# PEER block on one core: another division of the first choosing, gates stored in 16 pieces, and 47 chunks of the second u table split ahead of their use

## The reference, cut to what matters

```python
PEER_HEADS = 8; PEER_NK = 128; PEER_N = 16384; PEER_TOPK = 16; D_MODEL = 1024
def peer_ffn(h, wq, k1, k2, u, v):
    q = (ht @ wq).reshape(n_tok, PEER_HEADS, PEER_QDIM)
    s1 = einsum('thd,kd->thk', q[..., :128], k1); s2 = einsum('thd,kd->thk', q[..., 128:], k2)
    t1, i1 = top_k(s1, 16); t2, i2 = top_k(s2, 16)
    cand_s = (t1[..., :, None] + t2[..., None, :]).reshape(n_tok, 8, 256)
    top_s, pos = top_k(cand_s, 16)                    # 16 of 16384 experts for each token and head
    idx = take_along_axis(i1*128 + i2, pos); g = softmax(top_s)
    act = gelu(einsum('td,thkd->thk', h, u[idx]))     # u, v: 16384 rows of 1024
    return einsum('thk,thkd->td', g * act, v[idx])
```

## The kernel before

| | first layer | second layer |
|---|---|---|
| dense tiles | 4 | 3 |
| pre, ahead, beside | 16, 12, 16 | 16, 17, 19 |
| dots in the first choices, in one tile's 16 steps, in one later choice | 14, 44, 22 | 24, 24, 16 |
| gates of one tile are stored in | 4 pieces of 2 MB | 4 pieces of 2 MB |

## Time and profile before

### The profile page before, as it was taken

How to read it: one execution, slowest core, us unless ns; L and a number is a source line. 1 busy time by engine, 2 the same in 40 slices (tenths; PEclk the granted TensorE clock), 3 DMA queues, 4 the chain that set the end, 5 groups by cost and what they waited for, 6 DMA issues and landing times. The chain is left out here.

```text
span 4329.8 us, 59390 instructions
## 1 busy us (share of the span) xinstructions
PE 3731.4 (86%) x19545; PEld 1931.0 (45%) x19545; DVE 3186.7 (74%) x6186; ACT 1332.3 (31%) x1722; POOL 1663.6 (38%) x1191
## 2 busy tenths in 40 slices
PE   6888779789988898599999978877989888699996
PEld 1555565454434343344444424434545455344442
DVE  2547654539878788689999976843689788588887
ACT  0326521221212121222333305831334334333331
POOL 0400000230323232367887811203344344277774
PEclk8999989899999999899999989988999999899998
DMA  4946754596999998899999962212588797799995
GB/s 205 345 163 221 233 155 152 194 317 212 324 356 322 346 350 333 312 364 403 404 404 404 404 235 72 74 64 84 188 291 304 273 345 244 290 344 341 347 343 219
DMA packets 416426, 1188.55 MB, mean 275 GB/s; under 512 B 40112, under 2 KB 126960, under 8 KB 409584
## 3 DMA queue, kind: packets, MB, share of 16 engines
q1 hardware_dynamic: 240956, 639.75, 41.2%
q0 software_dynamic: 110592, 402.70, 25.7%
q10 hardware_dynamic: 64708, 143.91, 8.6%
HBM read 988.98 MB, written 197.23 MB: 274 GB/s over the span
## 5 line engine op out<-in xcount | busy, mean ns | idle before, releaser
L2097 PE MATMUL ex_R<-ex_vl,hh 128*128 128x512 f16 x1792 | 683.0, 381 | 0.0
L1665 PE MATMUL ca_A<-hh,ca_us 128*128 128x512 f16 x2048 | 634.3, 386 | 50.5 <-ACT ca_ga L1706 39.3
L2097 PE MATMUL ex_R<-hl,hh 128*128 128x512 f16 x1792 | 543.5, 382 | 93.8 <-DVE hh L2111 72.3
L1633 POOL DMA_INDIRECT ca_ug<-in_peer_u_rows,chosen_rows x288 | 293.9, 1020 | 660.6 <-DVE ca_ug L1790 538.7
L2128 DVE SCALAR_TENSOR_TENSOR ex_sum<-ex_vg,ex_share,ex_sum 128x1024 f32<-128x1024 f32 x384 | 493.4, 1285 | 9.8 <-DVE ex_share L2120 6.0
L2025 POOL DMA_INDIRECT ex_vg<-in_peer_v_rows,ex_index x384 | 388.5, 1012 | 190.3 <-issue 85.0
L1706 ACT ACTIVATE ca_ga<-ca_A 128x512 f32<-128x512 f32 (+1 forms) x256 | 139.4, 544 | 897.1 <-PE ca_A L1665 710.9
L1665 PE MATMUL ca_A<-hh,ca_uh 128*128 128x384 f16 x1024 | 345.5, 337 | 77.2 <-DVE ca_ul L1760 32.5
L1790 DVE SCALAR_TENSOR_TENSOR ca_ug<-ca_ug,ca_hp 128x1024 f32<-128x1024 f32 x288 | 346.7, 1216 | 84.4 <-DMA ca_ug<-in_peer_u_rows,chosen_rows 82.5
L1665 PE MATMUL ca_A<-hl,ca_us 128*128 128x512 f16 x1024 | 394.8, 386 | 0.0
L2136 DVE TENSOR_TENSOR ACC<-ACC,ex_R 128x512 f32<-128x512 f32 x448 | 305.8, 683 | 92.5 <-PE ex_R L2097 89.5
(11 more groups left out here) (384 smaller groups left out, 7126.4 us busy)
## 6 DMA issues: line engine op xcount, KB each, us to landing
ex_vr<-in_peer_v SPq DMA_DIRECT2D x256, 512.0 KB, 9.1
ca_us<-u_parts SPq DMA_DIRECT2D x128, 512.0 KB, 6.4
ca_ur<-in_peer_u SPq DMA_DIRECT2D x128, 512.0 KB, 5.2
gates<-ca_stage ACTq DMA_DIRECT2D x28, 2048.0 KB, 16.3
acts<-ca_ga ACTq DMA_DIRECT2D x128, 256.0 KB, 6.1
ex_gr<-gates SPq DMA_DIRECT2D x32, 1024.0 KB
ex_ar<-acts SPq DMA_DIRECT2D x128, 256.0 KB, 11.9
acts<-ca_ga ACTq DMA_DIRECT2D x128, 192.0 KB, 4.0
```

What stands on the lines that cost most here:

```text
L1633: nc.gpsimd.indirect_dma_start(ug[x % UG][:, :], None, u_rows, bass.IndirectOffsetOnAxis(ap=chosen_rows[:, x:x + 1], axis=0)).then_inc(ug_ ...
L1665: last = nc.tensor.matmul(A[b][:, a:a + w], lhs[:, k, :], rhs[:, k, a:a + w], start=(k == 0 and x == 0), stop=(k == KD - 1 and x == 2))
L2097: last = nc.tensor.matmul(R[(NP * q + y) % BANKS][:, :], lhs[q][:, x, o:o + P], rhs[q][:, x, h * 512:h * 512 + 512], start=(x == 0 and n = ...
```

## The change

Numbers of the schedule, in the first layer: `pre` 24 (was 16), `ahead` 11 (12), `beside` 15 (16); dots 20 in the second choice and 26 in the third (14 in the third), then 42 in a gate phase (44) and 14 in a choice phase (22). In the first choice that has dots, they begin when a fifth of its work is done. The places at which scores are loaded and exponentials made move by one to four chunks. In both layers `PARTS` is 16: pieces of 512 KB, spread over all the `ahead` chunks of a choice phase.

In the second layer 47 of the 128 chunks (x from 4 on with x % 8 in 0, 4, 6) are split ahead: 27 in `project_and_norm` n1 (5, 5, 5, 5, 3, 2, 2 in its 7 turns) and 20 in `peer_scores` (1, 1, 2, five times over). `choose_and_activate` loads those as pairs from DRAM, after the chunk that used the buffer before has been multiplied. Of the 81 others 4 are prefetched as before, and DVE subtracts all other 77; POOL subtracts none and only gathers. The prefetch of the 4 is issued by SP behind the stores of the split. Both SP's and ACT's loops in the second choosing are written out.

```diff
-    def __init__(self, nc, io, parts, first, raw, cut, raw_in, high_made, low_made, stored):
+    def __init__(self, nc, io, parts, layer, first, raw, cut, raw_in, high_made, low_made, stored):
+        self.chunks = READY[layer]
...
+READY = (range(PCH), [x for x in range(4, PCH) if x % 8 in (0, 4, 6)])
+SPLIT_NORM1 = (5, 5, 5, 5, 3, 2, 2)
+SPLIT_SCORES1 = (1, 1, 2) * 5
...
-                        rows.move(sp, 0, SPLIT_NORM, SPLIT_NORM)
-                        rows.all_stored(sp, SPLIT_NORM)
+                        rows.move(sp, 0, sum(split), sum(split))
+                        rows.all_stored(sp, sum(split))
...
-                        if rows is not None and i < SPLIT_NORM:
-                            rows.high(act, i)
+                        for x in range(sum(split[:i]), sum(split[:i + 1])) if rows is not None else ():
+                            rows.high(act, x)
...
+                        behind = 1 if tag == "n0" else 0
+                        for x in range(sum(split[:max(0, i - behind)]), sum(split[:i + 1 - behind])) if rows is not None else ():
+                            rows.low(dve, x)
...
-LOW_BY = (None, ("gpsimd", "vector", "gpsimd", "vector"))
...
+                    for j in range(SPLIT_RING if layer == 0 else 0):
+                        sp.dma_start(ring.us[j][:, :, :, :].rearrange("p x k n -> p (x k n)"), parts[j].rearrange("p x n -> p (x n)")).then_inc(ring.u_in[j], 16)
+                    for j in range(0 if layer == 0 else RING):
                         sp.dma_start(ring.ur[j][:, :, :], io["peer_u"][layer][j].rearrange("p (k n) -> p k n", k=KD)).then_inc(ring.u_in[j], 16)
+                    rows.all_stored(sp, upto[-1])
...
-PRE = (16, 16)
+PRE = (24, 16)
...
-    ahead, beside, midway_at = {4: (12, 16, 8), 3: (17, 19, 10)}[nt]
+    ahead, beside, midway_at = {4: (11, 15, 9), 3: (17, 19, 12)}[nt]
-    PARTS = 4
+    PARTS = 16
-    FIRST_DOTS, by_step, BY_CHOICE = {1: (24, [1, 2] * (STEPS // 2), 16), 2: (14, [3, 3, 2, 3] * (STEPS // 4), 22)}[NG]
+    first_dots, by_step, BY_CHOICE = {1: ((24,), [1, 2] * (STEPS // 2), 16), 2: ((20, 26), [3, 3, 2, 3, 2, 3, 2, 3] * (STEPS // 8), 14)}[NG]
...
-                        if last is not None and x % 2 == 0 and x // 2 < PARTS:
-                            store(last, x // 2)
+                        if last is not None:
+                            for part in range(PARTS * x // ahead, PARTS * (x + 1) // ahead):
+                                store(last, part)
...
+                    for x in range(RING, PCH):
+                        j = x % RING
+                        if x in ring.number:
+                            sp.wait_ge(first_done, x + 1)
+                            sp.dma_start(us[j][:, :, :, :].rearrange("p x k n -> p (x k n)"), parts[ring.number[x]].rearrange("p x n -> p (x n)")).then_inc(u_cut[j], 16)
+                            continue
+                        if x < 2 * RING:
+                            sp.wait_ge(first_cut, j + 1)
+                        else:
+                            sp.wait_ge(u_cut[j], ring.cut_upto[x - RING])
+                        sp.dma_start(ur[j][:, :, :], u_src[x].rearrange("p (k n) -> p k n", k=KD)).then_inc(u_in[j], 16)
...
-                        if low_by[j] == "gpsimd":
-                            pool.wait_ge(u_split, k * split_upto[-1] + split_upto[j])
-                            pool.wait_ge(first_done, k * RING + j + 1)
-                            nc.gpsimd.tensor_tensor(ul[j][:, :, :], ur[j][:, :, :], uh[j][:, :, :], ALU.subtract).then_inc(u_cut[j], 1)
...
-                        if not ready and low_by[j] == "vector" and not (isinstance(n, int) and n * CT + x < RING):
-                            dve.wait_ge(u_split, n * (CT // RING * split_upto[-1]) + (x // RING * split_upto[-1] + split_upto[j]))
+                        if not ready and n * CT + x >= RING and n * CT + x not in ring.number:
+                            dve.wait_ge(u_split, ring.split_upto[n * CT + x])
...
-                            while at["dots"] < dots_here * at["work"] // whole:
+                            lead = whole // 5 if first_dot == 0 else 0
+                            while at["dots"] < dots_here * (at["work"] - lead) // (whole - lead):
...
-                    for g in range(NG):
-                        choices(g, 0, g * (pre // NG), pre // NG, g)
+                    choices(0, 0, 0, pre // NG, 0)
                     dve.wait_ge(rows_ready, 1)
-                    choices(NG, 0, pre, ahead, None, 0, FIRST_DOTS)
+                    if NG > 1:
+                        choices(1, 0, pre // NG, pre // NG, 1, 0, first_dots[0])
+                    choices(NG, 0, pre, ahead, None, FIRST_DOTS - first_dots[-1], first_dots[-1])
```

More of the change, by code:

```diff
@@ L233, in load @@
             sp.wait_ge(self.low_made, i - len(self.raw) + 1)
-        sp.dma_start(self.raw[r], self.table[self.first + i]).then_inc(self.raw_in[r], 16)
+        sp.dma_start(self.raw[r], self.table[self.chunks[self.first + i]]).then_inc(self.raw_in[r], 16)
     def store(self, sp, i):
@@ L264, in table_split @@
 @contextmanager
-def table_split(nc, io, parts, first, tag, raw=(), cut=()):
+def table_split(nc, io, parts, first, tag, raw=(), cut=(), layer=0):
     with ExitStack() as c:
@@ L1335, in _ @@
                         weights(x)
-                        if rows is not None:
-                            rows.load(sp, x)
+                        rows.load(sp, x)
                     for x in range(N):
-                        if rows is not None and len(groups[x]):
+                        if len(groups[x]):
                             rows.move(sp, groups[x].start, groups[x].stop, upto[-1])
@@ L1636, in _ @@
                     issued = 0
-                    for x in range(0 if ready else PCH):
-                        if x >= RING:
-                            low(x // RING, x % RING)
-                        while issued < SLOTS and (pre if issued < UG else chunk_of_dot(issued - UG)) + 2 <= x:
-                            gather(issued)
-                            issued += 1
                     while issued < SLOTS:
```

105 lines of the change are left out of this document (40 added, 65 removed).

## The result

The changed kernel takes 4303.8 us, median of 6 runs (4296.3 to 4306.9), against 4328.5 for the kernel before on the same chip: ratio 0.9944, 95% interval 0.9932 to 0.9957. It is faster by 24.6 us; the forecast was 64.5 faster, 4264.5. The time lies in the range (4215 to 4312), and the sign is right; the size is not. The profiled execution has a span of 4304.8 us against 4329.8.

A forecast was written before the change was run, and what follows sets the result against it. Bounds: PE in the first choosing's begin, DMA in its choice phases, DVE in the second's gate phases. Terms: -39 first choosing, -62 second, +23 norm, +1.5 and +12 scores, -64.5 us in all; median 4264.5 us, range 4215 to 4312.

The forecast's parts named there:

- The sum went by DMA: First choosing, a period: 60 MB at 351 GB/s gives 171 us, taken as 169, against 192.2 before.
- the stores in small pieces spread over 11 chunks should keep ACT moving: First choosing, choice phases: ACT's 36.7 us wait for its own stores falls under 10 us; period taken as 169 us.
- 11 us of DVE's time in a gate phase: Second choosing: without POOL's subtractions DVE's one-hot operation (1381 ns, 692 in the first) gives back 11 us a gate phase.
- an unwaiting ACT in the choice phases: Second choosing: if DVE waits no more for ACT, choice phases take about 75 us against 91 and 88, 28 saved.
- five splits would fit into PE's 17 us of a turn: Second norm, until 2938: a turn's five splits, about 10 us with round trips, hide beside PE, costing nothing there.
- The first weights behind raw loads: Start of the scores: first weights share the queue with three raw loads of 512 KB, 1.5 us lost.
- The 20 splits hide beside PE, as the first layer's 30 did: Scores: the 20 splits run beside PE's products and cost nothing.
- a rival with 7%: Second choosing, SP's queue: raw loads behind pairs' loads come late, 2.5 us for each of 47 pairs, 4382 us; 7%.
- The late prefetch: End of the scores: four loads issued behind the last subtraction delay the last score copies, 12 us lost (ends 4 and 16).
- 12 more issues cost what they delay once their cover is gone: First choosing: ACT's 12 more DMA issues a tile lie beside 10 us of work; without it each delays a gelu.
- The pieces don't help: Both choosings: 16 pieces hold activation stores as long as 4; first gains nothing, second keeps 12 us of waits, 4315.5; 8%.
- The splits cost more: Norm and scores: round trips and prefetch at upper ends, plus a late store or load each turn, 4300 us; 10%.

The follow-up runs named there:

- e18: The kernel without splits (e10), gates in 4 pieces in both layers, issued behind chunks 0, 2, 4 and 6 of a choice phase: 4262.7 us, ratio 0.9843.
- e7: The kernel before with the first layer's part of the change alone, second layer as before: 4280.5 us, ratio 0.9890.
- e9: The kernel before with all 128 subtractions of the second choosing on DVE, none on POOL: 4308.7 us, ratio 0.9960.
- e19: The kernel before with all subtractions on DVE (e9), its 4 gate pieces spread over all chunks of a choice phase: 4262.0 us, ratio 0.9851.
- e15: The kernel without splits (e10), second layer's gates in 4 pieces and its exponentials and first dots as before: 4246.2 us, ratio 0.9811.
- e13: The kernel without splits (e10), second layer's gates in 4 pieces, still spread, first layer's in 16: 4236.5 us, ratio 0.9787.
- e10: The changed kernel with none of the 47 chunks split beside norm and scores, all else as changed: 4239.2 us, ratio 0.9798.
- e8: Built on e2, with five raw and five cut buffers in the second norm in place of three: 4253.4 us, ratio 0.9826.
- e1: The changed kernel with the second layer's weights x+3 issued in SP's queue ahead of the split's transfers: 4273.6 us, ratio 0.9873.
- e2: Built on e1, with the second choosing's four raw chunks loaded behind product 13's weights, cast and subtracted before the last splits: 4269.6 us, ratio 0.9865.
- e3: The changed kernel with the gates in 4 pieces in both layers, still spread over the phase: 4311.8 us, ratio 0.9958.

## Why the prediction was right and wrong

**First choosing: the size right, one reason of two.** Forecast 39, measured 43.8; begin 186.6 for 184.4, periods of 164 to 167 for 169, last gates 99 for 97. The sum went by DMA, 60 MB a period at 351 GB/s; the first period moved 96.8 x 341 + 67.3 x 377 = 58 MB, at 356. The step "the stores in small pieces spread over 11 chunks should keep ACT moving" is not borne out. The wait that it was to remove halved in the first choice phase (18.9 us for 36.7), but in the other two periods it is as long as before (before, 1307.3 to 1694 us, and changed, 1323.3 to 1656.7):

```profile
ACT ca_ga L1706 <- DMA acts<-ca_ga: 70.9, 11, 9.9
```

```profile
ACT ca_ga L1690 <- DMA acts<-ca_ga: 74.9, 17, 8.2
```

And e18 has periods of 168.2 us without small pieces or spread. The first layer alone gained a little more than its windows (e7).

**Second choosing: the size right, the shares wrong.** Forecast 62, measured 60.7. D fell by 55.2 us, and the kernels in between give: POOL's subtractions 16.7 (e9), the spread 19.2 (e19), the loops written out 1.1 (e15), the later exponentials and first dots 6.3 (e13), the pieces' size 0.9 (e10), the ready chunks 11.0 (changed). Taken in another order the exponentials give 9 and the spread 20. The prediction had the first (11 us of DVE's time in a gate phase) and an unwaiting ACT in the choice phases (28). It had no term for the exponentials, so that its sum came out within 2 us is in part luck, and it never asked what a ready chunk is worth by itself. That question would have been the one to ask: the whole cost of the change hangs on it.

**Norm: the mechanism right, the size short.** Forecast 23, measured 31.0. The prediction put nothing before the last product, since five splits would fit into PE's 17 us of a turn, 20 us between it and the last `hl`, and 3 to 5 for the last stores. Measured, the additions behind the first and the last products lie 57.1 us apart against 51.5, so 5.6 are lost where nothing was put; from there to the end of the last `hl` are 40.1 us against 22.9, 17.2 lost; and from there to the scores' first transfer 8.2 against 0.3, 7.9 lost. Five buffers (e8) bring these to 51.5, 32.2 and 6.7: of 32.6 us in B the round trips are 14. The first weights behind raw loads, put at 1.5, cost little: from the scores' first transfer to the first score copy are 21.2 us against 19.3, and kernels without splits in the second layer have 19.2 to 21.4 there.

**Scores: the step that failed.** Forecast 13.5, measured 41.3; this stretch has 27.8 of the 39.9 us by which the time missed the forecast. The prediction put the 20 splits at nothing: "The 20 splits hide beside PE, as the first layer's 30 did". Of the 39.3 us in C, 27.2 go when the weights are issued first (e1), some 20 of them PE's waits behind SP's queue and some 8 PE's own time at the lower granted clock behind these waits. I read the SP queue in the choosing (a rival with 7%) and not in the scores, where the order is the same. The first layer has the same order, and there SP's stores waited 100.5 us for DVE without PE waiting for POOL once. It has more time, seven pairs of products in 127 us (score copies from 831.4 to 958.1 us, before) against 86 here; that this is why is argued and not tested. The late prefetch, put at 12, is 7 (e2); 4.9 us stay (e2 against no splits).

**Behind the choosing**: nothing was forecast, 7.9 lost. Some 5 of it are the last tile's stores. From the start of the last step's one-hots to the end of the span are 637 to 640 us in ten kernels with 16 pieces in the second layer, and 633 to 634 in five with 4 pieces (e3, e13, e15, e18, e19). ACT's timeline there, e10 and then e13:

```profile
3603.69 18.21 ACTq L1715 DMA_DIRECT2D gates<-ca_stage  x16
3621.94 1.06 ACT L1683 ACTIVATE ca_us<-ca_ur 128x1024 f16<-128x1024 f32 x1 [18.29 <-issue]
```

```profile
3613.49 3.12 ACTq L1715 DMA_DIRECT2D gates<-ca_stage  x4
3616.66 1.06 ACT L1683 ACTIVATE ca_us<-ca_ur 128x1024 f16<-128x1024 f32 x1 [3.20 <-issue]
```

Sixteen issues in a row keep ACT from the next cast for 18.3 us, four for 3.2. The prediction said that 12 more issues cost what they delay once their cover is gone; here it is. The Trainium skill's rule to batch to 1 MiB or more (DMA: Bandwidth & Descriptors, Bandwidth) would have cost each choice phase 24 us by the estimate, made from the page's cost formula (Anatomy of one DMA — SWDGE (gpsimd) path), with one piece after another. The formula is fitted on DMAs issued by POOL, and here ACT issues them. The runs don't agree with the estimate: inside the phases small pieces are 1 to 6 us better in all of D, and a cost of this sort comes only at the end, so e13 with 4 pieces is as fast as e10.

**The rivals.** "The pieces don't help" was right in that small pieces by themselves give little, and that ACT waits as long for its stores (74.9 against 70.9 us in the later two periods). It was wrong in its time: the spread and the moved chunks gave the gain without them. "The splits cost more" (4300, 10%) is what happened, and its number lies 4 us off, in part by luck: it had round trips in the norm and a dearer prefetch, and not the weights, which cost most.

## What to carry to other kernels

Work moved ahead of a stage "for free" must be priced on every in-order queue that it shares: put the loads that the bound engine needs ahead of the side work's stores, whose waits run through two other engines. Before moving work, find what it is worth where it goes away, by leaving it out: here 11 us for 72. And large stores that are not urgent belong spread over the phase, not at its begin; with POOL's subtractions moved, these two lines took 47 us from the time (e9 to e19), more than the change. Where the chunks had been moved as well they gave less (26, e18 to e13).

## What the runs showed of the hardware

A DMA issue on ACT costs little alone (0.34 to 0.44 us in e10) and about 1.1 us each in a burst of 16 (18.2 us). Subtractions on POOL and DVE that run side by side stretch each other in the scores too: DVE's split takes 1.22 us alone and up to 3.14 beside POOL (changed). POOL's `sc_wl`, before (2127 ns), changed, and e1, where they overlap most:

```profile
L1363 POOL TENSOR_TENSOR sc_wl<-sc_w,sc_wh 128x1024 f16<-128x1024 f32 x14 | 29.8, 2127 | 1.1
```

```profile
L1371 POOL TENSOR_TENSOR sc_wl<-sc_w,sc_wh 128x1024 f16<-128x1024 f32 x14 | 34.9, 2494 | 1.1
```

```profile
L1373 POOL TENSOR_TENSOR sc_wl<-sc_w,sc_wh 128x1024 f16<-128x1024 f32 x14 | 40.5, 2893 | 1.1
```

TensorE's granted clock in the scores was 1.00, the upper of its two levels (2.4 GHz), as long as PE never waited (C before and in e10). In the changed kernel it was 0.86, 0.72 and 0.77, means over both levels, in stretches with PE's waits of 4.4, 7.1 and 4.8 us (3010 to 3022, 3034 to 3046, 3060 to 3075 us). And programs that differ only in the second layer differ in the first by up to 6 us a period; why was not tried.
